# PEER's second products with the tokens stationary and 512 columns moving

## What is computed

```
q = (xi @ w_query).reshape(B, T, PEER_HEADS, 2, PEER_HALF)
s = jnp.einsum('bthcd,cnd->bthcn', q, sub_keys)
...                               # top 16 of 16 x 16 pairs of keys: idx, softmax: gate
h = jax.nn.gelu(jnp.einsum('bthkd,btd->bthk', u_tab[idx], xi), approximate=False)
w = gate * h
return jnp.einsum('bthk,bthkd->btd', w, v_tab[idx])
```

## Time and profile before

| | us |
|---|---|
| median of three executions | 2098.24 |
| lowest, highest | 2094.31, 2099.83 |
| the profiled execution | 2098.77 |
| its span, first to last instruction | 2097.0 |
| mean granted clock of TensorE | 0.993 |

### The profile page before, as it was taken

The page is one execution under the profiler, slowest core; times in us unless marked ns, Lnnn a source line. Parts: engine busy times, 40 slices in busy tenths (PEclk is TensorE's granted clock), DMA queues, the critical chain, the costliest instruction groups (busy, mean ns, idle before and its releaser), DMA issues. The chain is left out here.

```text
span 2097.0 us, 37760 instructions
## 1 busy us (share of the span) xinstructions
PE 2048.8 (98%) x13979; PEld 1889.4 (90%) x13979; DVE 1626.9 (78%) x3108; ACT 1221.9 (58%) x2557; POOL 1065.9 (51%) x604
## 2 busy tenths in 40 slices
PE   8899999999999999999999999999999999999999
PEld 8789998888999999877999888899999988997888
DVE  8658987785699998666699777659999878557776
ACT  6555577776555555655456777655555555555443
POOL 2217987778577771001698777757777315000000
PEclk9999999999999999999999999999999999999999
DMA  5145665555799998553566555569999856335554
GB/s 173 52 156 170 201 198 174 180 181 182 250 355 359 362 363 270 152 160 120 165 201 192 177 176 178 189 212 350 365 360 363 309 178 218 101 122 171 191 191 151
DMA packets 151095, 451.78 MB, mean 215 GB/s; under 512 B 20720, under 2 KB 25584, under 8 KB 150912
## 3 DMA queue, kind: packets, MB, share of 16 engines
q1 hardware_dynamic: 127936, 381.64, 55.4%
q0 software_dynamic: 22688, 67.72, 8.8%
q10 hardware_dynamic: 288, 0.01, 0.0%
HBM read 439.14 MB, written 9.44 MB: 214 GB/s over the span
## 5 line engine op out<-in xcount | busy, mean ns | idle before, releaser
L250 ACT ACTIVATE hi<-raw 128x1024 fp32r<-128x1024 f32 (+2 forms) x705 | 738.6, 1048 | 401.7 <-PE bank L1494 102.2
L259 POOL TENSOR_TENSOR lo<-raw,hi 128x1024 fp32r<-128x1024 f32 x256 | 620.7, 2430 | 195.6 <-ACT hi L250 195.0
L259 DVE TENSOR_TENSOR lo<-raw,hi 128x1024 fp32r<-128x1024 f32 (+2 forms) x449 | 544.0, 1215 | 178.9 <-ACT hi L250 178.1
L1529 PE MATMUL bank<-pe_middle,hi 128*128 128x384 f32 x2048 | 415.5, 344 | 11.4 <-DVE pe_middle L1842 10.5
L1529 PEld LDWEIGHTS bank<-pe_middle,hi 128*128 128x128 f32 x2048 | 348.1, 189 | 19.2 <-DVE pe_middle L1842 18.6
L1483 PE MATMUL bank<-xx,hi 128*128 128x512 f32 x1176 | 305.9, 399 | 0.0
L1494 PEld LDWEIGHTS bank<-xx,lo 128*128 128x128 f32 x2048 | 269.4, 188 | 13.8
L1494 PE MATMUL bank<-xx,lo 128*128 128x256 f32 x2048 | 280.5, 280 | 0.0
L1534 PE MATMUL bank<-pe_middle,lo 128*128 128x192 f32 x2048 | 266.8, 271 | 0.0
L1534 PEld LDWEIGHTS bank<-pe_middle,lo 128*128 128x128 f32 x2048 | 265.7, 191 | 0.0
L1610 POOL DMA_INDIRECT pe_seen<-pe_aside,pe_picks x128 | 200.6, 1567 | 118.3 <-DVE pe_sums_aside L1855 60.7
(11 more groups left out here) (431 smaller groups left out, 3424.2 us busy)
## 6 DMA issues: line engine op xcount, KB each, us to landing
raw<-in_peer_u SPq DMA_DIRECT2D x256, 512.0 KB, 3.5
raw<-in_peer_v SPq DMA_DIRECT2D x256, 512.0 KB, 5.7
raw<-in_w_gate_up SPq DMA_DIRECT2D x44, 512.0 KB, 4.3
raw<-in_w_in SPq DMA_DIRECT2D x34, 512.0 KB, 4.3
raw<-in_gla_w_in SPq DMA_DIRECT2D x24, 512.0 KB, 4.2
raw<-in_w_down SPq DMA_DIRECT2D x22, 512.0 KB, 4.3
raw<-in_w_query SPq DMA_DIRECT2D x16, 512.0 KB, 3.5
pe_aside<-pe_stage SPq DMA_DIRECT2D x32, 256.0 KB, 4.3
```

The source lines that it names most:

```text
L250: act.activation(k.hi[:, n % RING, at_hi:at_hi + x * e], k.raw[:, n % RAW, 0:x * e], ACT.Copy).then_inc(k.hi_done, 1)
L259: eng.tensor_tensor(k.lo[:, n % RING, at_lo:at_lo + x * e], k.raw[:, n % RAW, 0:x * e], k.hi[:, n % RING, at_hi:at_hi + x * e].bitcast(F32 ...
L1529: pe.matmul(k.bank[V_BANK[c]][:, 0:2 * TD], cols, middle[:, v % 2].rearrange("p s t -> p (s t)"), start=(v == 0), stop=False, skip_group_c ...
```

## The change

The second products are turned over. The middle values are stationary and the slab's halves of 512 columns move, so the sums stand as tokens x columns, in four banks (`second_ps`). For the first 128 tokens: high and low middle values x high half, high x low half. For the last 64 of the 192 one operand of 128 columns holds their low and high middle values side by side (`weights`, a = 1), and goes with the high and with the low half; its bank then holds the low sums in partitions 0 to 63 and the high ones in 64 to 127. For the last TAIL = 5 slabs the two are separate products of 64 rows again. Before these five, ACT copies partitions 64 to 127 aside (`lift`), a DMA on POOL's queue moves them to partitions 0 to 63, and DVE adds them to h (`add_moved`). Copies, joins and transposes at the end are gone; DVE adds each bank to h when its last product is done (`first_part`).

ACT makes a second copy of 64 columns of the high middle values in each slab. The slabs' low halves lie without the offset of 16 (SKEW). Picks stand at 8 + 7n/4 instead of 10 + 25n/16, the merge at 124 instead of 115. The last `put_aside` is issued by ACT right behind its GELU. POOL fetches the first four rows before it waits for the stores; values are fetched four picks at a time and multiplied by the gates four at a time.

```diff
@@ -181,7 +181,7 @@
         for i in range(NK):
-            add_slab(k, k.dram["peer_v"][l, i].unsqueeze(1), 1, D, k.lo_dve, (0, SKEW))
+            add_slab(k, k.dram["peer_v"][l, i].unsqueeze(1), 1, D, k.lo_dve)
         if l == 0:
...
@@ -1291,11 +1291,12 @@
 LATER = ("squared", "rooted", "opened")
-BOTH = ("q_act", "q_dve", "summed", "powered", "turned", "gated", "added", "mixed")
+BOTH = ("q_act", "q_dve", "summed", "powered", "turned", "gated", "mixed")
 V_ORDER = ((0, 0), (1, 0), (0, 1), (1, 1))
-V_BANK = (4, 5, 6, 7, 3, 2, 0, 1)
-PICK_AT = {10 + n * 25 // 16: n for n in range(PICKS)}
-MERGE_AT = 115
+TB = TD - P
+TAIL = 5
+PICK_AT = {8 + n * 7 // 4: n for n in range(PICKS)}
+MERGE_AT = 124
 GROUP_AT = {slab_of(g): g for g in range(GROUPS)}
...
@@ -1335,7 +1337,7 @@
         gate_16 = k.sb(ctx, "pe_gate_16", [P, TD], F16)
-        middle = k.sb(ctx, "pe_middle", [P, 2, 2, TD], F32R)
+        middle = k.sb(ctx, "pe_middle", [P, 2, 2 * TD + TB], F32R)
         count = k.sb(ctx, "pe_count", [P, NK], I32)
...
@@ -1344,8 +1346,8 @@
         weight = k.sb(ctx, "pe_weight", [P, PICKS])
-        low_sums = hidden[:, 0:KD, :]
-        sums_t = hidden[:, KD:2 * KD, :]
+        upper = hidden[P - TB:P, 32:38, :].rearrange("p i t -> p (i t)")[:, 0:D]
+        lower = hidden[0:TB, 32:38, :].rearrange("p i t -> p (i t)")[:, 0:D]
         others = hidden[:, 2 * KD:2 * KD + 14, :].rearrange("p i t -> p (i t)")
...
@@ -1428,7 +1424,7 @@
                         place_picks()
-                    if 0 <= i < NK and i % STAGED == STAGED - 1:
+                    if 0 <= i < NK - 1 and i % STAGED == STAGED - 1:
                         put_aside(i // STAGED)
...
@@ -1523,29 +1519,36 @@
-                def high(v, c):
-                    cols = hi[:, (v0 + v) % RING, c * P:(c + 1) * P]
-                    pe.matmul(k.bank[V_BANK[c]][:, 0:2 * TD], cols, middle[:, v % 2].rearrange("p s t -> p (s t)"),
-                              start=(v == 0), stop=False, skip_group_check=True)
-                def low(v, c):
-                    return pe.matmul(low_sum(c), lo[:, (v0 + v) % RING, SKEW + c * P:SKEW + (c + 1) * P],
-                                     middle[:, v % 2, 0], start=False, stop=(v == NK - 1), skip_group_check=True)
+                def weights(v, a, low):
+                    if a == 1 and v < NK - TAIL:
+                        return middle[:, v % 2, 2 * TD - TB:2 * TD + TB]
+                    at = low * TD + a * P
+                    return middle[:, v % 2, at:at + (P if a == 0 else TB)]
+                def product(v, a, c, low, w, **flags):
+                    rows = P if a == 0 or v < NK - TAIL else TB
+                    return pe.matmul(second_ps(a, c)[0:rows], weights(v, a, low), w[:, (v0 + v) % RING, c * 512:(c + 1) * 512],
+                                     skip_group_check=True, **flags)
+                def highs(v, a, c):
+                    product(v, a, c, 0, hi, start=(v == 0), stop=False)
+                    if a == 0 or v >= NK - TAIL:
+                        product(v, a, c, 1, hi, start=False, stop=False)
...
                     pe.wait_ge(k.hi_done, v0 + v + 1)
-                    for part in (range(0, 5), range(5, KD)) if v == 0 else (range(KD),):
-                        for c in part:
-                            if v == 0 and V_BANK[c] < 3:
-                                pe.wait_ge(gated.sem, gated_before(NK - 1 - (NK - 1 - V_BANK[c]) % 3))
-                            high(v, c)
-                        pe.wait_ge(*k.lo_at[v0 + v])
-                        for c in part:
-                            last = low(v, c)
+                    for c in range(2):
+                        for a in range(NT):
+                            highs(v, a, c)
+                    pe.wait_ge(*k.lo_at[v0 + v])
+                    for c in range(2):
+                        for a in range(NT):
+                            last = product(v, a, c, 0, lo, start=False, stop=False)
                     last.then_inc(k.eaten, 1)
...
@@ -1554,19 +1557,10 @@
                     pe.wait_ge(*k.lo_at[v0 + v])
-                    for c in range(KD):
-                        high(v, c)
-                        low(v, c).then_inc((joined.sem if c < KD - 1 else k.eaten), 1)
-                def turn_back():
-                    for a, half in V_ORDER:
-                        pe.wait_ge(added.sem, added.at(4 * half + 4))
-                        tok = slice(a * P, min((a + 1) * P, TD))
-                        for x in range(4):
-                            last = pe.transpose(second_ps(a, half)[0:tok.stop - tok.start, x * P:(x + 1) * P],
-                                                sums_t[:, 4 * half + x, tok], k.ident[:])
-                        last.then_inc(returned.sem, 1)
+                    for n, (a, c) in enumerate(V_ORDER):
+                        highs(v, a, c)
+                        product(v, a, c, 0, lo, start=False, stop=True)\
+                            .then_inc((first_part.sem if n < 3 else k.eaten), 1)
...
@@ -1591,33 +1585,45 @@
                 last_second()
-                turn_back()
                 after.raise_all(pe)
...
             def _(pool):
+                def fetch_values(n):
+                    for m in range(n, n + FOUND):
+                        pool.indirect_dma_start(seen[:, m:m + 1], None, aside.rearrange("j i t -> (j i t)").unsqueeze(1),
+                                                bass.IndirectOffsetOnAxis(ap=picks[:, 1, m:m + 1], axis=0))\
+                            .then_inc(valued.sem, 16)
+                def fetch_row(n):
+                    pool.indirect_dma_start(found[:, n % FOUND], None, v_rows,
+                                            bass.IndirectOffsetOnAxis(ap=picks[:, 0, n:n + 1], axis=0),
+                                            element_offset=l * NK * NK * D).then_inc(picked[n % FOUND].sem, 16)
                 pool.memset(keys, 0.0).then_inc(zeroed.sem, 1)
...
                 pool.wait_ge(placed.sem, placed.at(16 * ASIDE))
+                for n in range(FOUND):
+                    fetch_row(n)
                 for x in range(2):
                     pool.wait_ge(written[x].sem, written[x].at(8 * NK // STAGED))
-                for n in range(PICKS):
-                    if n >= FOUND:
-                        pool.wait_ge(mixed.sem, mixed.at(n - FOUND + 1))
-                    pool.indirect_dma_start(seen[:, n:n + 1], None, aside.rearrange("j i t -> (j i t)").unsqueeze(1),
-                                            bass.IndirectOffsetOnAxis(ap=picks[:, 1, n:n + 1], axis=0))\
-                        .then_inc(picked[n % FOUND].sem, 16)
-                    pool.indirect_dma_start(found[:, n % FOUND], None, v_rows,
-                                            bass.IndirectOffsetOnAxis(ap=picks[:, 0, n:n + 1], axis=0),
-                                            element_offset=l * NK * NK * D)\
-                        .then_inc(picked[n % FOUND].sem, 16)
+                fetch_values(0)
+                for n in range(PICKS - FOUND):
+                    pool.wait_ge(mixed.sem, mixed.at(n + 1))
+                    fetch_row(n + FOUND)
+                    if n % FOUND == 0:
+                        fetch_values(n + FOUND)
                 pool.wait_ge(mixed.sem, mixed.at(PICKS))
...
                         .then_inc(merged.sem, 16)
+                pool.wait_ge(lifted.sem, lifted.at(2))
+                pool.dma_start(lower, upper).then_inc(moved.sem, 16)
                 after.roots(pool)
...
@@ -1652,6 +1658,9 @@
                     last.then_inc(bent.sem, 1)
+                    if i == NK - 1:
+                        act.wait_ge(bent.sem, bent.at(NK))
+                        act.dma_start(aside[:, STAGED * b:, :], stage[:, b % 2]).then_inc(written[b % 2].sem, 16)
...
@@ -1679,15 +1688,13 @@
                         act.wait_ge(k.eaten, v0 + v - 1)
-                    act.activation(middle[:, v % 2, 0], hidden[:, v], ACT.Copy).then_inc(m_hi.sem, 1)
-                def keep_low_sum(c):
-                    if c < KD - 1:
-                        act.wait_ge(joined.sem, joined.at(c + 1))
-                    else:
-                        act.wait_ge(k.eaten, end)
-                    act.activation(low_sums[:, c], low_sum(c), ACT.Copy).then_inc(halved.sem, 1)
+                    act.activation(middle[:, v % 2, 2 * TD:], hidden[:, v, P:TD], ACT.Copy)
+                    act.activation(middle[:, v % 2, 0:TD], hidden[:, v], ACT.Copy).then_inc(m_hi.sem, 1)
+                def lift(c):
+                    act.wait_ge(k.eaten, v0 + NK - TAIL)
+                    act.activation(upper[:, c * 512:(c + 1) * 512], second_ps(1, c)[TB:P], ACT.Copy).then_inc(lifted.sem, 1)
...
@@ -1721,8 +1728,9 @@
                             split_middle(i - NK + 2)
-                for c in range(KD):
-                    keep_low_sum(c)
+                    if n == V0 + NK - TAIL:
+                        lift(0)
```

(48 more changed lines are left out.)

## The result

The changed kernel takes 2101.85 us (median of 20 runs, 2097.93 to 2107.21), the kernel before, run beside it, 2098.07 (2094.08 to 2103.91): 1.002 times as long, interval 1.0012 to 1.0028. Forecast were 2088 us and "faster"; it is slower, by less than the 0.3% that I had called no change. The time lies inside the full range, 2072 to 2106, but outside the 2082 to 2098 of my own case.

The account below looks back on a forecast made before the run. In the second products DVE with PE was taken as the limit, then DMA. Per layer -3.5 - 0.2 + 1.8 - 0.9 - 2.5 = -5.3, -10.6 for two, from 2098.8 to about 2088 us; range 2072 to 2106.

Parts of the forecast that it names:

- my own case: Whole kernel: the summed steps hold, about 2088 us, own range 2082 to 2098; chance 0.55.
- rival B: Second products: rows leaving POOL within 4 us make slab loads late; 0.33 a cycle gives 2098 us; chance 0.18.
- part 1: Second products on PE: ten products take 2.283 us a slab, 0.017 less; last slabs add 1.8 a layer.
- the end of the layer: From last slab's start to last addition to h: 3.6 us instead of 6.16, so -2.5 a layer.
- a slab of 2.35 without picks: Sign in the second products' plain slabs, forecast 2.28 apart: this length would make part 1 wrong.
- Part 5: POOL's row and value fetches, last store, dropped skew: taken at 0, bound +1.6 us a cycle.
- rival A: Second products: a row lands late each cycle and DVE waits; 1.0 a cycle gives 2120 us; chance 0.14.
- Parts 3 and 4: Merge at slab 124 saves 0.9 us a layer, lifts and transfer cost 0; the layer's end saves 2.5.
- The level of before: Old slabs among picks: 2.403 us each in layer 1, second layer called the same pattern; 267.7 for 112 slabs.
- Part 2: Slabs among picks: ACT's copy adds 0.14, DVE's work falls to 2.12; 2.359 us a slab, -3.5 a layer.
- tail: Last five slabs: 12 products, 2.74 us; 0.44 more in each of slabs 123 to 126, +1.8 a layer.

Follow-up runs that it names:

- 2: The changed kernel with the stationary tile of middle values moved by 16 columns (64 bytes a partition); 2096.96 us in one execution.
- 12: The changed kernel with the stationary tile of middle values moved by 64 columns (256 bytes); 2105.64 us in one execution.
- 5: As 2, but one value fetched with each row, eight picks ahead, instead of four in a block; 2092.87 us in one execution.
- 6: As 2, but rows 4 to 63 of a layer not fetched, the first four mixed again and again; 2086.97 us in one execution.
- 10: The kernel before with its own products, plus the change's pick places, early first rows, values in blocks and ACT store; merge at 122; 2100.83 us, ratio 1.0007.
- 11: As 10, but values fetched one with each row, eight picks ahead; 2092.79 us, 0.9972 of the kernel before.
- 13: The same program as 2, timed repeatedly; 2099.18 us, 1.0008 of the kernel before.
- 9: As 5, with the merge at slab 122; 2094.48 us, 0.9977 of the kernel before.
- 3: The changed kernel with products of one PSUM bank side by side and the low half waited for at the slab's start; 2108.11 us in one execution.
- 4: The changed kernel with TAIL 64 instead of 5, so 64 slabs have 12 products; 2146.62 us in one execution.
- 14: The changed kernel with values fetched one with each row, eight picks ahead, tile in its old place; 2098.03 us, 1.0009 of the kernel before.

## Why the prediction was wrong

Forecast were 10.6 us less, measured 3.8 more. Two steps failed above all: the sum took the slabs' own loads at nothing beside rows that leave in a burst (rival B; 3 to 4 us a layer), and part 1 took 2.283 for a slab that lasts 2.333 (2 to 3 us a layer). A third, the end of the layer, took 1.1 more than forecast.

**Part 1, the products: the step failed.** "I take 2.283, the same form." The form was the same, the addresses were not. Measured 2.333, above even the upper bound of 2.31 that the earlier trace rows gave. Shown by 2 and 12: 64 bytes restore 2.287, 256 bytes don't. The prediction had named "a slab of 2.35 without picks" as what would refute it; 2.333 with nothing late comes short of that figure but is past the bound. The Trainium skill (TensorE: Matmul & The Clock Gate, "Back-to-back issue gap") has a formula for the isolated gap that depends on the column count alone, 215.8 ns at 512. The trace has neither that value nor one value for the count: 233.3 and 228.7 ns at the same count and clock. The price in time is 0.5 a layer in the plain slabs and, by changed kernel less 2, 0.6 among the picks in layer 1 and 2.2 in layer 2; it isn't the main part.

**Part 5 and rival B: the likelier failure had 0.18.** "Taken at 0, the bound is +1.6 us a cycle" was for rows. The rows did land in time (median 8.0 us, at most 10.0), and in the changed kernel DVE waited for none of them, and once, 0.6 us, for values: rival A didn't happen, POOL being held 1.10 at the median by a value instead of 1.95. What came late were the slabs, as B had it, by the mechanism it named. My case against B was the mean demand of 349 GB/s and the 2.7 us of the earlier trace rows; but the mean says nothing of three rows within 4.4 us. Shown by 5 and 6, and by 10 against 11. It cost 4.0 us a layer by 2 less 6, and 3.1 by 13 less 6: 0.2 to 0.25 a cycle where B had reckoned with 0.33. So B alone would not have made the change slower; it took the other misses as well.

**Parts 3 and 4, merge and end: mis-sized.** "The transfer of 256 KB and its addition end before the last slab does. Cost 0; bare, the addition would be 1.22." Not the transfer but DVE's own order was late: merge, middle values, a low half for the next stage, then that addition. So the end is 4.76, not 3.6, nearly the bare addition's 1.22. Merge and last slabs otherwise took 11.46 where 11.36 was forecast, and the lifts 0.59 each where I took 0.6.

**The level of before.** I took layer 1's 2.403 for both layers and called the second's row "the same pattern"; but its 99 slabs in 236.00 are 2.384 each. Over the same 110 slabs, merge included, layer 2 took 263.1 before where layer 1 took 264.4. That is 0.65 a layer of gain that was never there.

**Part 2, ACT and DVE: right.** ACT's second copy costs the 0.14 forecast. In a plain slab that starts at 838.31, DVE's middle values start 0.81 and the low half 1.75 later (0.80 and 1.75 forecast):

```profile
838.57 0.26 ACT L1691 ACTIVATE pe_middle<-pe_hidden 128x64 fp32r<-128x64 f32 x1 [0.86 <-PE bank L1532]
838.73 0.35 ACT L1692 ACTIVATE pe_middle<-pe_hidden 128x192 fp32r<-128x192 f32 x1
838.99 1.04 ACT L250 ACTIVATE hi<-raw 128x1024 fp32r<-128x1024 f32 x1
...
839.12 0.36 DVE L1850 TENSOR_TENSOR pe_middle<-pe_hidden,pe_middle 128x192 fp32r<-128x192 f32 x1
840.06 1.23 DVE L259 TENSOR_TENSOR lo<-raw,hi 128x1024 fp32r<-128x1024 f32 x1 [0.59 <-ACT hi L250]
```

The sum of a layer, means over both: late slabs and rows 4.0 (2 less 6), pace 1.5 among the picks (changed kernel less 2) and 0.5 in the plain slabs, end 1.1, level of before 0.65, tail 0.1, and 0.6 by which even 6 is above the forecast and that no run parts further: 8.45 of the 8.5 missed. That it closes so well is partly luck. With 13, the same program as 2, the first two terms are 3.1 and 2.4, and by the medians a layer missed 7.2 rather than 8.5. Which terms are large is shown; their sizes are good to 1 us.

## What to carry to other kernels

The pace of a form of product holds for its operands' addresses too: where ten plain products take longer than the same form elsewhere, move the stationary tile by 64 bytes and measure again, before arguing about order or skew. Where the DMA engines are 0.95 busy, count the bytes that leave within one transfer's landing time, not those of a whole cycle; the same fetches spread evenly were worth 8.0 us here (10 against 11), the products' new shape nothing that could be measured (9 against 11). At the end of a stage write out the queue of the engine that adds last, with the next stage's work in it.

## What was not expected of the hardware

- 512 columns, clock 1.00: products start 238 and 229 ns apart by turns, with the tile 64 bytes further 225 to 236 (mean 228.7), with 256 bytes further 238 and 229 again. What lies behind it is open: whether the first slot, the second or a tile behind them has to move, and why 3, 4 and 14, with the tile in its old place, showed an order of 228 to 242 with a mean of 232.4 instead of the alternation's 233.3.
- A value's indirect fetch holds POOL 0.94 to 2.59 us for the same 128 small reads, 1.10 at the median in blocks of four, 1.95 singly ahead of each row and 1.69 singly behind each row in 5 and 11:

```profile
L1595 POOL DMA_INDIRECT pe_seen<-pe_aside,pe_picks x128: 940/1100/2586, 554.2 to 1665.9; - x128
```
